# Two transformer blocks on one core: dilated attention issued in pieces between the steps of RWKV's chunked scan, and the first norm's squares split over three engines

## What is computed

```python
def rmsnorm(x, g):
    y = xf * lax.rsqrt(jnp.mean(xf * xf, axis=-1, keepdims=True) + EPS)
    return y.astype(x.dtype) * g
```

```python
ATTN_GROUPS = ((128, 1), (512, 4), (2048, 16))      # (window, dilation), two heads each

def dilated_window_attention(q, k, v, window, dilation):
    scores = jnp.einsum('bnqrhe,bnkrhe->bnrhqk', qb, kb) * (e ** -0.5)
    scores = jnp.where(mask[None, :, None, None], scores, -jnp.inf)
    mx = jnp.max(scores, axis=-1, keepdims=True)
    p = jnp.exp(scores - mx)
    den = jnp.sum(p, axis=-1, keepdims=True)
    out = jnp.einsum('bnrhqk,bnkrhe->bnqrhe', p / den, vb)
    lse = (mx + jnp.log(den))[..., 0]
    return out, lse

def dilated_mixture_attention(p_attn):
    ...
    alpha = jax.nn.softmax(jnp.stack(lses, axis=0), axis=0)
    o = jnp.concatenate([o_g * alpha[g][..., None] for g, o_g in enumerate(outs)], axis=2)

def wkv7_scan(r, w, k, v, a, b):                    # per head, state is 64 x 64
    def step(state, inp):
        sa = jnp.einsum('bhij,bhj->bhi', state, a_t)
        state = state * w_t + sa * b_t + v_t * k_t  # outer products
        return state, jnp.einsum('bhij,bhj->bhi', state, r_t)
```

## Time and profile before

| quantity | value |
| --- | --- |
| time, median of 3 runs (lowest, highest) | 2960.38 us (2959.85, 2961.13) |
| the profiled execution's own time | 2978.22 us |
| its span (first to last instruction) | 2976.4 us |
| TensorE busy, share of the span | 2856.7 us, 96% |
| mean granted TensorE clock, 1.0 is 2.4 GHz | 0.977 |
| attention, first to last: its first matmul to RWKV's first | 2127.5 to 2198.5 us |
| RWKV's loop | 2198.5 to 2297.7 us |

### The profile page before, as it was taken

The page is one execution under the profiler, slowest core; times in us unless marked ns, Lnnn a source line. Parts: engine busy times, 40 slices in busy tenths (PEclk is TensorE's granted clock), DMA queues, the critical chain, the costliest instruction groups (busy, mean ns, idle before and its releaser), DMA issues.

```text
span 2976.4 us, 37041 instructions
## 1 busy us (share of the span) xinstructions
PE 2856.7 (96%) x14900; PEld 2246.8 (75%) x14900; DVE 1500.8 (50%) x2096; ACT 992.6 (33%) x1495; POOL 235.6 (8%) x208
## 2 busy tenths in 40 slices
PE   7999998899999999999889999999979999999998
PEld 6888775488887888877648888877668566788887
DVE  4343564643345443356464344566555895443444
ACT  4222432532223422233263222453324112322223
POOL 1000021010000000002101000001000550100000
PEclk9999999999999999999999999999779999999999
DMA  3323221023222222223103222222100122223222
GB/s 132 105 89 106 81 100 50 1 96 105 88 100 91 95 93 100 93 85 113 51 1 128 88 97 96 88 85 73 66 2 4 58 68 68 92 88 103 89 95 85
DMA packets 52042, 241.87 MB, mean 81 GB/s; under 512 B 6024, under 2 KB 6344, under 8 KB 31584
## 3 DMA queue, kind: packets, MB, share of 16 engines
q1 hardware_dynamic: 50096, 233.38, 22.9%
q10 hardware_dynamic: 1440, 6.77, 0.6%
q0 software_dynamic: 400, 0.23, 0.0%
HBM read 238.34 MB, written 2.10 MB: 81 GB/s over the span
## 4 chain that ended last, share of the span: by engine, by line
PE 84%; DVE 10%; ACT 3%; issue 1%; POOL 1%; DMA 1%; SPq 0%; POOLq 0%; DVEq 0%; ACTq 0%; PEldq 0%
PE psum L475 83%; DVE ring_lo L1711 2%; DVE stat L1915 1%; PE psum L797 1%; DMA ring<-in_wmix 1%; POOL scr L2469 1%; ACT highs L1270 0%; DVE scr L1923 0%; DVE highs L1711 0%; DVE hid L1904 0%; ACT highs L1337 0%; DMA x<-in_x 0%; DVE scr L1900 0%; DVE scr L1902 0%; DVE hid_r L1711 0%
## 5 line engine op out<-in xcount | busy, mean ns | idle before, releaser
L475 PE MATMUL psum<-highs 128*128 128x512 f32 (+1 forms) x3776 | 1331.3, 390 | 28.7 <-DVE ring_lo L1711 18.5
L475 PE MATMUL psum<-highs,ring_lo 128*128 128x512 f32 (+1 forms) x2696 | 1034.1, 391 | 0.0
L475 PEld LDWEIGHTS psum<-highs 128*128 128x128 f32 x3776 | 706.8, 188 | 187.8 <-issue 38.2
L475 PE MATMUL psum<-h_lo,highs 128*128 128x512 f32 x1952 | 761.7, 390 | 0.0
L1711 DVE TENSOR_TENSOR ring_lo<-ring,highs 128x2048 fp32r<-128x2048 f32 (+3 forms) x163 | 354.8, 2179 | 776.7 <-ACT highs L1337 702.4
L475 PEld LDWEIGHTS psum<-highs,ring_lo 128*128 128x128 f32 (+1 forms) x2696 | 507.2, 188 | 108.2 <-issue 0.5
L475 PEld LDWEIGHTS psum<-h_lo,highs 128*128 128x128 f32 x1952 | 367.1, 188 | 77.2 <-issue 0.5
L1337 ACT ACTIVATE highs<-ring 128x2048 fp32r<-128x2048 f32 x110 | 206.5, 1877 | 563.0 <-DMA ring<-in_wgu 539.0
L1711 DVE TENSOR_TENSOR highs<-hid,highs 128x512 fp32r<-128x512 f32 x220 | 157.4, 716 | 205.7 <-ACT highs L1364 113.2
L2469 POOL TENSOR_TENSOR scr<-scr 128x512 f32<-128x512 f32 x52 | 83.0, 1595 | 1755.3 <-ACT scr L1295 1753.1
L475 PE MATMUL psum<-highs,wdr_lo 128*128 128x512 f32 x488 | 190.0, 389 | 0.0
(11 more groups left out here) (390 smaller groups left out, 2910.6 us busy)
## 6 DMA issues: line engine op xcount, KB each, us to landing
ring<-in_wgu SPq DMA_DIRECT2D x105, 1024.0 KB, 4.9
wdr<-in_wd SPq DMA_DIRECT2D x110, 256.0 KB, 2.7
ring<-in_wd SPq DMA_DIRECT2D x25, 1024.0 KB, 4.8
ring<-in_wmix SPq DMA_DIRECT2D x22, 1024.0 KB, 4.9
ring<-in_wmix SPq DMA_DIRECT2D x24, 704.0 KB, 4.1
ring<-in_wproj SPq DMA_DIRECT2D x22, 512.0 KB, 3.6
ring<-in_wgu SPq DMA_DIRECT2D x10, 512.0 KB, 5.4
mixw<-in_wsmall ACTq DMA_DIRECT2D x3, 1280.0 KB, 5.5
```

Source lines behind the costliest of these rows:

```text
L475: return nc.tensor.matmul(o, w, r, start=start, stop=stop, skip_group_check=True)
```

## The change

**Attention in pieces.** Two heads of one group and one query tile form a unit, so there are 12 instead of 24. A unit uses bank 6 or 7 alone for scores, transposes and output in turn. Its steps are tied to slots: slot 27t + i stands behind step i of tile t, and the eight steps of unit k stand at slots 5k, 5k+1, 5k+2, 5k+3, 5k+5, 5k+6, 5k+7, 5k+8. TensorE issues a piece after its slot's RWKV step; VectorE and ScalarE issue theirs before the next RWKV step whose source stands at or behind the slot. The division by the row sum is gone from the unit: the output is copied unscaled (new, `d_numerator`), and the scale is put into the mixing of the groups, for which the maxima are spread as well as the log sums (48 matmuls instead of 24, in six pieces), GpSimd adds and multiplies six times, and VectorE's long reciprocal is cut into four.

**Transposes among the projections.** The 60 transposes are issued between and behind the last six projections instead of behind all.

**S5's tables** of powers go between RWKV's steps of tile 0 on VectorE.

**The start.** GpSimd squares tiles 0 to 3, ScalarE squares 4 to 7, VectorE adds. ScalarE itself waits for x. TensorE has 12 matmuls of 128 x 256 on a constant tile at its start, whose results nobody reads.

**DMA.** Of the first four gate weights SP now loads two after `su1`, and the third and fourth only once attention's result is complete (`attn_y`), since its buffers lie there.

The diff, cut to its core:

```diff
@@ tables
-            + ["ak0", "ak1", "ak2", "av0", "av1", "av2", "su0", "su1", "av0t", "av1t", "av2t"]
-            + [f"t{n}{t}" for n in "ABKV" for t in range(NT)])
+            + ["ak0", "ak1"] + [f"tA{t}" for t in range(NT)] + ["ak2"] + [f"tB{t}" for t in range(NT)]
+            + ["av0"] + [f"tK{t}" for t in range(NT)] + ["av1", "av2", "av0t", "av1t", "su0", "su1", "av2t"]
+            + [f"tV{t}" for t in range(NT)])
...
+D_EVEN, D_ODD, D_MAX, D_EXP, D_TURN, D_COPY, D_ATTEND, D_PUT = (
+    {5 * k + o: k for k in range(PAIRS)} for o in (0, 1, 2, 3, 5, 6, 7, 8))
+D_LOGS, D_LSE = 64, 65
+D_SPREAD = {66: 0, 67: 1, 69: 2, 70: 3, 72: 4, 73: 5}
...
+D_TOP, D_BELOW, D_WEIGHT, D_TOTAL, D_SHARE = 76, 77, 79, 82, 84
...
@@ SyncE
-                if q < 4:
+                if q < 2:
                     sp.wait_ge(made, NUM["su1"] + 1)
+                elif q < 4:
+                    sp.wait_ge(attn_y, 3)
...
@@ TensorE
+            for _ in range(12):
+                mm(psum[:, 3, 0:2 * P], ident, cst[:, 0:2 * P], True, True)
...
+            def d_score(k, e):
+                g, i = divmod(k, NT)
+                n, r = d_keys(k), slice(HD * e, HD * e + HD)
+                if e:
+                    pe.wait_ge(scores, D0 + 2 * k + 1)
+                elif k >= 2:
+                    pe.wait_ge(d_put, k - 1)
+                o = d_bank(k)[:, 2 * P * e:2 * P * e + n * P]
+                mm(o, dq[r, g, i * P:(i + 1) * P], dk[r, g, (i + 1 - n) * P:(i + 1) * P], True, False)
...
+            def d_turn(k):
+                pe.wait_ge(expd, D0 + 2 * k + 2)
+                for e in range(2):
+                    for t in range(d_keys(k)):
+                        c = slice(2 * P * e + t * P, 2 * P * e + t * P + P)
+                        last = nc.tensor.transpose(d_bank(k)[:, c], dprobs[k % 2][:, c], ident)
+                last.then_inc(turned, 1)
...
+            def d_attend(k):
+                pe.wait_ge(pt_put, D0 + k + 1)
+                for t in range(n):
+                    kt = i + 1 - n + t
+                    for e in range(2):
+                        last = mm(d_bank(k)[HD * e:HD * e + HD, 0:P], dv[g][:, kt * P + HD * e:kt * P + HD * e + HD],
+                                  dpt[k % 2][:, 2 * P * e + t * P:2 * P * e + t * P + P], t == 0, t == n - 1)
...
                     for p in range(3):
                         rw_step(name, t, p)
+                    at = slot(name, t)
+                    if at in D_ATTEND:
+                        d_attend(D_ATTEND[at])
+                    if at in D_TURN:
+                        d_turn(D_TURN[at])
+                    if at in D_EVEN:
+                        d_score(D_EVEN[at], 0)
+                    if at in D_ODD:
+                        d_score(D_ODD[at], 1)
+                    if at in D_SPREAD:
+                        d_spread(D_SPREAD[at])
...
@@ ScalarE, VectorE: before each of their RWKV steps
+                    upto = slot(ACT_SOURCE.get(name, name), t) + 1
+                    for at in range(reached, upto):
+                        attention(at)
+                    reached = upto
...
@@ GpSimd
+            for g in range(3):
+                nc.gpsimd.tensor_tensor(max_of[g], max_of[g], top, ALU.add).then_inc(d_pool, 1)
+            for g in range(3):
+                pool.wait_ge(d_wexp, 4 + g)
+                nc.gpsimd.tensor_tensor(yt[g], yt[g], max_of[g], ALU.mult).then_inc(d_pool, 1)
```

365 lines of the change are left out of this document (214 added, 151 removed).

## The result

The changed kernel takes 2941.91 us (median of 7 runs, 2929.63 to 2947.92) for 2962.36 of the kernel before in the same rounds: ratio 0.9911, 95% interval 0.9885 to 0.9938. It is faster by 0.9%, as forecast in sign, but by 18.5 us against the 2960.38 that the forecast starts from, or 20.5 against the 2962.36 of the same rounds, where 49.2 were forecast, and it is outside the range of 2888 to 2934. The seven runs of the kernel before lie at 2959.9 to 2962.4 (four) and at 2979.1 to 2981.3 (three). Its profiled execution took 2938.70 us for 2978.22, so 39.5 less from profile to profile.

What follows compares the result with a forecast made beforehand. TensorE, busy 96% of the span, was taken as the bound. The loop's end 41.3 us earlier plus the start's 7.9 made 49.2 off 2960.4, so 2911 us, range 2888 to 2934.

Steps and rivals of the forecast that it cites:

- the distance that I kept between profile and median: In the final sum: the profiled execution lies 17.8 us above the median of the runs, and stays so after the change.
- its full 76.1 us: Ahead of RWKV: without attention's own stretch, RWKV starts at 2122.4 instead of 2198.5, minus 76.1 us.
- the mixing at the border of tiles 2 and 3 and the tables in tile 0: In RWKV's loop: this work is covered by attention's own matmuls, adding nothing, or up to 15 us if not covered.
- my 96.4: RWKV's loop without attention: four tiles of 24.1 us at full clock, 96.4 us.
- the start: Program start: row sums at 23.5, product at about 24.5, 5.9 us from the wait and 2.0 from clock, minus 7.9.
- TensorE's pieces: Attention's matmuls in RWKV's loop: 37.6 us added, changes of shape included, less 6 us that fill TensorE's waits.
- what follows the loop: Behind RWKV's loop: stays the same; nothing taken for the later loads of the third and fourth gate weights.
- RWKV's start: RWKV's first matmul comes at 2122 less the start's 8, near 2114.
- 0.5 us a burst for 12 bursts, 6 us: In the loop: ScalarE's attention bursts delay evacuations that TensorE needs, 6 us in all.
- (C): Rival: in-order queues bind, half of the 61 us moved to ScalarE and VectorE delays TensorE; 2941 or 2942; chance 0.17.
- (B): Rival: changes of shape cost nothing beside RWKV, ScalarE and VectorE delay nobody; loop 110.9, time 2888 us; chance 0.17.
- (D): Rival: the loop falls to 1.2 GHz because TensorE stands at each piece; loop 256, time about 3033 us; chance 0.02.

Runs made afterwards that it cites:

- pool_later: The changed kernel with GpSimd's three additions waiting for VectorE's three subtractions, so they no longer run together; 2935.54 us, ratio 0.9884 to the kernel before.
- pe_pieces: The changed kernel with attention's TensorE matmuls in the loop but no waits for other engines, whose attention work is left out; 2934.49 us, ratio 0.9877.
- mix_between: spread_and_later with VectorE's subtractions behind RWKV's U of tile 2, ScalarE's exponentials and the sum moved later too; 2930.16 us, ratio 0.9888.
- no_pieces: The changed kernel without any of attention's work in RWKV's loop, its outputs zeros written by GpSimd; 2906.67 us, ratio 0.9771.
- shapes: no_pieces plus unread work behind every slot: one 128 x 128 transpose in tile 1, three in tile 2, four 64 x 64 matmuls in tile 3; 2928.02 us.
- same_shape: no_pieces plus unread work behind every slot: one 64 x 64 matmul in tile 1, two in tile 2, one 128 x 128 transpose in tile 3; 2909.30 us.
- tables_spread: The changed kernel with S5's tables moved out of tile 0 on VectorE, partly ahead of the loop, partly into tile 1; 2934.37 us, ratio 0.9879.
- spread_and_later: The changed kernel with both edits, those of tables_spread and pool_later; 2934.49 us, ratio 0.9881.
- mix_later: spread_and_later with the groups' mixing pulled apart and taken one by one in the middle of tile 3; 2942.15 us, ratio 0.9926.

## Why the prediction was wrong

The miss is 2941.9 - 2911.2 = 30.7 us. It splits as 17.8 + 9.7 + 3.2: the distance that I kept between profile and median, the miss from profile to profile, and the changed kernel's median lying 3.2 above its own profile.

**The step that failed first** is in the sum: "it lies 17.8 above the median of the runs, and I keep that distance". A distance can be kept only if it belongs to something that stays. This one lay in attention's stretch, the very part that I removed at its full 76.1 us: 71.0 us in two profiles of the kernel before, 52.7 in the third. For an execution near 2960 only some 58 us (76.1 less 18.3) were there to remove. That those executions had the short stretch is inferred, from the two groups of times and the estimate above, and not traced. Page and times had both numbers, 2978.2 and three runs within 1.3 us near 2960, and the row at a clock of 0.53 was the one place in the rows big enough for the difference.

**The step that failed second**: "the mixing at the border of tiles 2 and 3 and the tables in tile 0 I take as covered by attention's own matmuls, with up to 15 us if they are not". They were not. The loop without pieces took 104.0 for my 96.4, nearly all of it in tile 0 with the tables, and the other engines' attention 9.2: 5.9 in tile 2 (39.6 for 33.7), where the mixing stood, and 3.4 in tile 0 (44.5 for 41.1). Of these 3.4 most is the clock: pool_later, with the same tile 0 and as little of it at the low level as pe_pieces, is 1.1 above it (42.2 for 41.1). The shares of busy time that I argued from, at most 61% in each tile of the kernel before, were true, and said nothing of the two places where TensorE's next step waits for the row behind.

**Right in place and size:** the start (row sums at 23.8 for 23.5, the following product at 24.59 for 24.5, and zero for the unread matmuls); TensorE's pieces, 29.7 for 31.6, though the change of shape is 0.15 to 0.18 an entry where the sum has 0.1 for most; and what follows the loop, 0.9 us off. RWKV's start, 1.5 us late, is right in part by luck: with the same order of TensorE ahead of it, it lies anywhere from 2111.8 (mix_between) to 2122.2 (no_pieces), with 27.3 to 54.6 us at the low level between 60 and 2095. **Right only by sum:** the "0.5 us a burst for 12 bursts, 6 us" on ScalarE. The term was to cover delays by the other engines, which came to 9.2, but they did not come from bursts spread over the loop: tile 1 is 0.1 us longer with its bursts than without, and tile 0, with the larger ones of two key tiles, at most 1.1 at a like clock.

Of the rivals, (C) forecast the number, 2941 or 2942, with a loop of 164.5 us; the loop was 142.9. Its loop is 21.6 too long, about as much as the kept distance and the changed kernel's own, 17.8 + 3.2, took off on the other side, and its mechanism, 30.5 us of moved work landing on TensorE's path, is excluded by pe_pieces, which leaves 9.2. (B), changes of shape for nothing, is excluded by shapes and same_shape. (D), the loop at 1.2 GHz, came in small: 17 us of the loop at the low level. In tile 0 6.8 us of it are worth 2.3 (44.5 for 42.2) or 2.8 (40.3 for 37.5), so by an estimate from these two the 10.2 of the changed kernel cost 3.4 to 4.2.

Open: what decides whether attention's stretch in the kernel before gets the low clock or not. Two of its three profiles have it, one has not, and 21 of the 72 timed runs were in the upper group. Open too is what makes the clock fall in tile 0: tables_spread has 6.8 us of it, and spread_and_later, mix_later and mix_between, with the same work in tile 0, have none.
